# Seven quadrant products in place of eight for the feed-forward input stages of a two-block network on one core

## What is computed

```python
SEQ, D_MODEL, D_FF = 512, 1024, 2816

def swiglu_ffn(x, w_in, w_out):
    gate, up = jnp.split(x @ w_in, 2, axis=-1)      # w_in: 1024 x 5632
    return (jax.nn.silu(gate) * up) @ w_out         # w_out: 2816 x 1024

h = h + 0.5 * swiglu_ffn(rmsnorm(h, norm_ffn1[l]), ffn1_w_in[l], ffn1_w_out[l])
...                                                  # mixer: retention and pooling, or convolution and delta rule
h = h + 0.5 * swiglu_ffn(rmsnorm(h, norm_ffn2[l]), ffn2_w_in[l], ffn2_w_out[l])
```

## Time and profile before

| | |
|---|---|
| median of 3 runs | 2215.12 us (2214.97 to 2216.24) |
| span of the profiled execution | 2213.7 us |
| PE busy | 2198.3 us, 99% of the span |
| DVE busy | 1071.2 us, 48% |
| ACT busy | 748.3 us, 34% |
| POOL busy | 439.2 us, 20% |

### The profile page before, as it was taken

The page is one execution under the profiler, slowest core; times in us unless marked ns, Lnnn a source line. Parts: engine busy times, 40 slices in busy tenths (PEclk is TensorE's granted clock), DMA queues, the critical chain, the costliest instruction groups (busy, mean ns, idle before and its releaser), DMA issues.

```text
span 2213.7 us, 26476 instructions
## 1 busy us (share of the span) xinstructions
PE 2198.3 (99%) x10012; PEld 1820.3 (82%) x10012; DVE 1071.2 (48%) x1126; ACT 748.3 (34%) x1000; POOL 439.2 (20%) x343
## 2 busy tenths in 40 slices
PE   8999999999999999999999999999999999999998
PEld 6888888888777888888888888888788888888887
DVE  6444334453466545444444544443588866444322
ACT  5232222232233334222232422223472354232222
POOL 1222101620123002222211222230002003222101
PEclk9999999999999999999999999999999999999999
DMA  4322234333222232233333223233322123233232
GB/s 147 95 97 101 95 105 133 95 115 100 81 79 74 87 99 99 96 95 95 95 107 111 92 99 95 95 105 105 110 71 67 53 82 95 95 99 100 95 105 96
DMA packets 60255, 213.54 MB, mean 96 GB/s; under 512 B 6688, under 2 KB 9120, under 8 KB 59936
## 3 DMA queue, kind: packets, MB, share of 16 engines
q1 hardware_dynamic: 59616, 209.50, 29.5%
q0 software_dynamic: 288, 2.62, 0.3%
q10 hardware_dynamic: 288, 0.52, 0.1%
HBM read 210.52 MB, written 2.10 MB: 96 GB/s over the span
## 4 chain that ended last, share of the span: by engine, by line
PE 97%; issue 1%; DVE 0%; DMA 0%; POOL 0%; ACT 0%; SPq 0%; POOLq 0%
PE acc L541 30%; PE acc L543 30%; PE acc L542 30%; PE mixb L1022 1%; PE mixb L1045 1%; PE acc L984 1%; PE acc L983 1%; PE acc L982 1%; PE mixb L867 0%; PE acc L878 0%; PE mixb L878 0%; DMA w_raw<-weights 0%; PE acc L867 0%; PE sums L788 0%; PE sums L592 0%
## 5 line engine op out<-in xcount | busy, mean ns | idle before, releaser
L541 PE MATMUL acc<-x_hi,w_hi 128*128 128x512 f32 x2016 | 792.7, 393 | 7.8 <-DVE x_lo L1528 7.8
L543 PE MATMUL acc<-x_hi,w_lo 128*128 128x512 f32 x2016 | 786.0, 390 | 0.0
L542 PE MATMUL acc<-x_lo,w_hi 128*128 128x512 f32 x2016 | 785.7, 390 | 0.0
L541 PEld LDWEIGHTS acc<-x_hi,w_hi 128*128 128x128 f32 x2016 | 379.2, 188 | 86.7 <-DVE x_lo L1528 8.8
L543 PEld LDWEIGHTS acc<-x_hi,w_lo 128*128 128x128 f32 x2016 | 379.0, 188 | 79.7
L542 PEld LDWEIGHTS acc<-x_lo,w_hi 128*128 128x128 f32 x2016 | 379.4, 188 | 77.5
L1509 DVE TENSOR_TENSOR w_lo<-w_raw,w_hi 128x1024 fp32r<-128x1024 f32 x231 | 298.0, 1296 | 232.7 <-ACT w_hi L1095 231.7
L1621 DVE TENSOR_TENSOR w_lo<-w_raw,w_hi 128x1024 fp32r<-128x1024 f32 x160 | 246.3, 1539 | 271.0 <-ACT w_hi L1101 271.0
L1095 ACT ACTIVATE w_hi<-w_raw 128x1024 fp32r<-128x1024 f32 x231 | 242.1, 1054 | 286.6 <-DMA w_raw<-weights 286.6
L541 PE MATMUL acc<-hid_hi,w_hi 128*128 128x512 f32 (+1 forms) x726 | 277.9, 383 | 0.0
L542 PE MATMUL acc<-hid_lo,w_hi 128*128 128x512 f32 (+1 forms) x726 | 277.7, 383 | 0.0
(11 more groups left out here) (363 smaller groups left out, 1749.7 us busy)
## 6 DMA issues: line engine op xcount, KB each, us to landing
w_raw<-weights SPq DMA_DIRECT2D x391, 512.0 KB, 3.4
y_t<-h SPq DMA_DIRECT2D x16, 128.0 KB, 1.8
h<-x_t SPq DMA_DIRECT2D x3, 512.0 KB, 6.8
k1c<-const POOLq DMA_DIRECT2D x1, 1536.0 KB, 9.2
k2c<-const POOLq DMA_DIRECT2D x1, 1024.0 KB, 7.8
h<-x_t ACTq DMA_DIRECT2D x2, 256.0 KB, 4.0
w_raw<-weights SPq DMA_DIRECT2D x1, 384.0 KB, 5.2
cst<-const SPq DMA_DIRECT2D x1, 161.0 KB, 8.4
```

The lines of the kernel that those rows point to most:

```text
L541: pe.matmul(bank, w_hi[:, slot, w], hi, start=start, stop=False)
L542: pe.matmul(bank, w_hi[:, slot, w], lo, start=False, stop=False)
L543: return pe.matmul(bank, w_lo[:, slot, w], hi, start=False, stop=stop)
```

## The change

An input stage now works on a double: two gate tiles and two up tiles of 128 features at once, 11 doubles a part (6 and then 5, `HALVES`). The four weight tiles that face a pair of input tiles are seen as a 2x2 matrix of quadrants, and the tokens are cut into two halves of 256. The 2x2 by 2x2 product is made with seven products of quadrants instead of eight (Winograd's form of Strassen's scheme). So a double has seven blocks of 24 matmuls with 256 columns, named `P1 P6 P2 P7 P5 P4 P3` in their order, where there were four blocks of 24 matmuls with 512 columns.

What this needs besides:

- DVE makes four sums of weight blocks per double (`weight_sum`, s1 to s4, 128x1024 each), and splits seven blocks rather than four.
- The input tiles are combined too: `xc_hi` and `xc_lo` hold seven combinations of 256 tokens for each of four pairs of tiles. `combine` on ACT and DVE makes them once ahead of each part, in place of `x_hi` and `x_lo`.
- Three PSUM areas `r_a`, `r_b`, `r_c` of two half banks hold running sums of products. ACT copies P1 to `f_s`; DVE takes seven steps of 512 elements to get gate and up from the areas (counted by `quad`; `made(d, "u2")` and so on name them). PE may start P7 only when the step `u2` has read `r_b`, P4 after `u3`, P3 after `c22`.
- Silu (ACT), the product `hid_f` (DVE, `hidden`) and `hid_hi` (ACT) are now 128x1024, once per double. POOL makes `hid_lo` alone, one instruction of 128x1024 per double, and `f_mul` is gone; `rstd` enters the up side when the output is added to `h` instead.
- The output stage runs in two passes, after 6 doubles and after 5, in 12 and 10 full blocks; each of the eight tiles is drained and added to `h` in both (`add_tile`, two DVE instructions, where there was one in all).
- Weights have eight slots. The hardware loops are gone, all blocks are written out.

```diff
-PHASES = [("ffn0_in", 2 * KF), ("ffn0_out", 3 * KD), ("pool_in", 4), ...
+PHASES = [("ffn0_in0", 42), ("ffn0_out0", 12), ("ffn0_in1", 35), ("ffn0_out1", 10), ("pool_in", 4), ...
+PRODUCTS = ("p1", "p6", "p2", "p7", "p5", "p4", "p3")
+P1, P6, P2, P7, P5, P4, P3 = range(7)
+B11, B21, B22, T2, U3, U1, U4 = range(7)
+COMBO = (B11, T2, B21, U3, U1, U4, B22)
+HALVES = (6, 5)
...
+NORM_AT = {0: P2, 1: P6, 2: P6, 3: P6}
...
+            def quadrants(f, d, n0, before, fresh):
+                for i, x in enumerate(COMBO):
+                    n = n0 + i
+                    take_block(n)
...
+                    if i == P2:
+                        pe.wait_ge(f_acted, 2 * d + 1)
+                        bank = r_a
+                    if i == P7:
+                        pe.wait_ge(quad, made(d, "u2"))
+                        bank = r_b
+                    if i == P5:
+                        if d:
+                            pe.wait_ge(quad, made(d - 1, "c12"))
+                        bank = r_c
+                    if i == P4:
+                        pe.wait_ge(quad, made(d, "u3"))
+                        bank = r_b
+                    if i == P3:
+                        pe.wait_ge(quad, made(d, "c22"))
+                        bank = r_c
...
+                    for u in range(2):
+                        for k in range(KD // 2):
...
+                            last = product(n, 4 * u + k, bank[:, u, :], xc_hi[:, k, x, :], xc_lo[:, k, x, :],
+                                           opens and k == 0, k == KD // 2 - 1, read_between=True)
+                    last.then_inc(block_done, 1)
...
+            def hidden(d):
+                dve.wait_ge(f_acted, 2 * d + 2)
+                if d:
+                    dve.wait_ge(hid_done, 2 * d)
+                dve.tensor_tensor(hid_f[:, hid_of(d), :], f_up[:, :, :], f_gate[:, :, :], ALU.mult).then_inc(hid_done, 1)
...
+                        before(n0 + P2)
+                        if not fresh:
+                            hidden(d - 1)
+                        split(n0 + P2)
...
+                        prepare(n0 + P7)
...
+                        dve.wait_ge(block_done, n0 + P6 + 1)
+                        dve.tensor_tensor(f_gate[:, :, t2], r_b, f_s[:, :, :], ALU.subtract).then_inc(quad, 1)
+                        prepare(n0 + P5)
...
-                        pool.wait_ge(f_sig_done, q + 1)
-                        pool.tensor_tensor(f_mul[:, u, :], f_sig[:, u, :], rstd[:, :], ALU.mult).then_inc(f_mul_done, 1)
-                        pool.wait_ge(hid_hi_done, q + 1)
-                        pool.tensor_tensor(hid_lo[:, 2 * i + u, :], f_hid[:, u, :], hid_hi[:, 2 * i + u, :].bitcast(F32),
-                                           ALU.subtract).then_inc(hid_done, 1)
+                    pool.wait_ge(normed, WIDE["norm3"] + 1)
                     for m in range(KD):
                         pool.tensor_tensor(h[:, m, :], h[:, m, :], r_one[:, :], ALU.mult).then_inc(h_final, 1)
+                for d in range(sum(HALVES) * f, sum(HALVES) * (f + 1)):
+                    pool.wait_ge(hid_hi_done, d + 1)
+                    pool.tensor_tensor(hid_lo[:, hid_of(d), :], hid_f[:, hid_of(d), :], hid_hi[:, hid_of(d), :].bitcast(F32),
+                                       ALU.subtract).then_inc(hid_done, 1)
```

More of the change, by code:

```diff
@@ new lines, with tile_end, _take @@
+TILE_ENDS = [[m for m in range(8) if OUT_END[p][m] % 8 != 7] for p in range(2)]
+def tile_end(f, p, m):
+    g = OUT_END[p][m]
+    if g % 8 == 7:
+        return "block", FIRST[f"ffn{f}_out{p}"] + g // 8 + 1
+    return "tile", f * (len(TILE_ENDS[0]) + len(TILE_ENDS[1])) + (len(TILE_ENDS[0]) if p else 0) + TILE_ENDS[p].index(m) + 1
+BUFFERS = 8
+RAW, LO, LOADS, LOADED, FREED = {}, {}, [], {}, {}
+_free = {slot: -1 for slot in range(BUFFERS)}
+_times = {slot: 0 for slot in range(BUFFERS)}
+def _take(name, load, slots=BUFFERS):
+    slot = min(range(slots), key=lambda s: (_free[s], s))
+    if load:
+        LOADS.append((slot, _free[slot]))
+        _times[slot] += 1
+        LOADED[name] = (slot, _times[slot])
+    else:
+        FREED[name] = _free[slot]
+    after, _free[slot] = _free[slot], NB
+    return slot
@@ new lines, in out_tiles @@
+            def out_tiles(f, p):
+                first, out0, ds = FIRST[f"ffn{f}_out{p}"], OUT0[f"ffn{f}_out{p}"], [d for d, n0 in doubles(f, p)]
+                for g, (m, k) in enumerate(OUT_SEQ[p]):
+                    if f == 3 and p == 1 and m == KD - 1:
+                        if k == 0:
+                            last_tile(g, first, out0 + m)
+                        continue
+                    n = first + g // 8
+                    if g % 8 == 0:
+                        take_block(n)
+                    if k == 0:
+                        if m < 2:
+                            pe.wait_ge(quad, made(ds[-1], "c11"))
+                        elif m < 4:
+                            pe.wait_ge(quad, made(ds[-1], "c21"))
+                        else:
+                            pe.wait_ge(drained, out0 + m - 3)
+                    if m == 0 and k % 2 == 0:
+                        pe.wait_ge(hid_done, 2 * (ds[0] + k // 2) + 2)
+                    last = product(n, g % 8, acc[m % 4], hid_hi[:, k, :], hid_lo[:, k, :], k == 0, k == 2 * HALVES[p] - 1)
+                    if g % 8 == 7:
+                        last.then_inc(block_done, 1)
+                    elif g == OUT_END[p][m]:
+                        last.then_inc(tile_done, 1)
@@ L651, in last_sum @@
+            def ffn(f):
+                for p in range(2):
+                    for i, (d, n0) in enumerate(doubles(f, p)):
+                        quadrants(f, d, n0, OUT0[f"ffn{f}_in{p}"], i == 0)
+                    out_tiles(f, p)
             def last_sum(t):
@@ L1189, in ffn @@
-                split(first + 2 + LEAD)
-                for u in range(2):
-                    act.wait_ge(drained, out0 + 2 * u + 1)
-                    act.activation(f_sig[:, u, :], f_gate[:, u, :], ACT.Silu).then_inc(f_sig_done, 1)
-                    if u:
-                        split(first + 2 * u + 1 + LEAD)
-                    act.wait_ge(drained, out0 + 2 * u + 2)
-                    act.activation(hid_hi[:, u, :], f_hid[:, u, :], ACT.Copy).then_inc(hid_hi_done, 1)
-                with act.Fori(1, 2 * KF // SLOTS) as i:
-                    turn_of(i)
@@ L2392 @@
     arrays = {
-        "weights": np.concatenate(list(_weights(v))).reshape(NB, P, TILES * P),
+        "weights": np.concatenate([w.reshape(-1, P, TILES * P) for w in _weights(v)]),
         "x_t": np.ascontiguousarray(v["x"][0].T.reshape(KD, P, S).transpose(1, 0, 2)),
```

846 lines of the change are left out of this document (503 added, 343 removed), and 3 rows, old and new, of the table PHASES.

## The result

The changed kernel takes 2302.2 us (median of 4, 2301.74 to 2304.48) where the kernel before takes 2215.3 (2214.97 to 2216.24): 1.039 times as long, 95% interval 1.038 to 1.041. The forecast was 2242, with a range up to 2268. Its direction was right, and its size was 60 us short. The profiled execution has a span of 2299.9 us, against 2213.7.

The account below looks back on a forecast made before the run. PE, busy 99%, was taken as the bound. From 2213.7 us: -71.3 PE's stream, +47.9 ordinary doubles, +24 part 0, +9.2 parts 1 and 3, +17.7 part 2; 2241.2, with 1.4 for the median 2242 us, range 2190 to 2268.

Parts of the forecast that it names:

- What bounds it, and PE's stream: Whole kernel: PE is the bound; input stages' matmuls fall from 957.6 to 886.3 us, 71.3 us less.
- the rival by which each weight load shows: Input stages: weight loads do not overlap, 0.213 us a matmul, 2834 us in all; chance 0.01.
- The ordinary double: 36 doubles: P7 waits for `u2`, delayed by POOL's `hid_lo`; 1.33 us each, 47.9 in all, bounds 0 and 61.
- So 0.7 to 0.9 of what is left.: DVE step starting inside a POOL instruction loses this share of its remainder; the split of P7 loses 1.9 of 2.4 us.
- Eight first doubles, second passes: First doubles after each start have no `hidden`, so no such loss; second passes of output have room on DVE: 0 us.
- Part 0: Start of the first part: input mixing and DVE's order delay the first blocks, 24 us (18 to 30).
- Parts 1, 2 and 3: Starts, counted from the last tile of `h`: 4.6 us each for parts 1 and 3, 17.7 for part 2.
- The products of `h` by `r_one`: Start of part 2: POOL's eight products, moved there from the end of the input stage, cost 6 us.
- The tail: End of the kernel: loses one add of 0.4 us, saves 72 matmuls' fixed 0.013 us; counted as 0.
- POOL misses the split: Rival, ordinary double: POOL starts inside the split of P7 and waits, so P7 is on time; 2194 us, chance 0.22.
- works as meant: Rival, whole kernel: the design works and the starts are hidden too; 2144 us, chance 0.04.
- DVE behind for good: Rival, doubles: DVE's own sum exceeds PE's, 22 us a double; 2262 us, up to 2280; chance 0.12.

Follow-up runs that it names:

- e1: The changed kernel with DVE instead of POOL making `hid_lo`, just ahead of step c12: 2239.6 us.
- e2: The changed kernel with POOL making `hid_lo` in two instructions of 512 elements instead of one of 1024: 2261.9 us.
- e4: The changed kernel with DVE doing the sum s1 after `u2` instead of ahead of the split of P7: 2272.7 us.
- e5: The changed kernel with ACT's rounding of the inner tiles, which releases POOL, moved behind the split of P5's weights: 2239.2 us.
- f4: e1 with DVE instead of POOL adding the squares for the norms ahead of parts 1, 2 and 3: 2220.5 us.
- f1: e1 with ACT rounding the next output block's weights earlier, ahead of the tile's square, in output stages ahead of parts 1 to 3: 2225.4 us.
- f2: e1 with POOL's sums of squares ahead of parts 1 to 3 cut to 16 columns of 512, leaving most out: 2215.5 us.
- g1: e1 with the edits of f1 and f4 together: 2213.6 us, 0.9993 of the kernel before.
- f3: e1 with POOL's eight products of `h` by `r_one` at the start of part 2 cut to 16 columns of 512: 2234.5 us.

## Why the forecast was wrong in size and right in kind

**What bounds it, and PE's stream: right.** 256-column matmuls with a weight load each keep their 0.120 us in the loops: seven blocks of 24 take 20.16 us in e1, 20.14 forecast. The 71.3 us are there in every kernel, and the rival by which each weight load shows (0.213 us a matmul, 2834 us) is out.

**The ordinary double: the mechanism was right, the term mis-sized.** The step that failed: "So 0.7 to 0.9 of what is left." I read three losses as a fraction and took 0.8 of 2.4. They are no fraction. In the rows that I had, the losses are 0.37, 1.09 and 1.07 with 0.51, 1.23 and 1.21 us of POOL's left: each time what is left less 0.14. After the change it is the same: 2.35 left, loss 2.21; in e2 1.24 and 1.11; in e4 and e5 1.75 and 1.61. The DVE instruction does its work when POOL's has ended. For 2.4 us left that makes 2.26, not 1.9; 2.35 were left and 2.21 lost, 0.3 us a double more than forecast. The rest of the 0.46 by which a double was missed is the gap from the end of `u2` to P7 (0.14) and 0.03 for PE's own stream and the order. "Here POOL starts 0.4 inside s1 and loses 0.3" had it on the wrong engine: s1 takes its 1.22, and POOL, which came second, is the one held, by 0.46 (2.86 us where one alone takes 2.40 at 1202.38).

The upper bound, 1.7 us, was exceeded (1.79), because it was built with 0.9 of what is left. e1 and e5 show that the cause is this overlap and its place, not DVE's amount of work: both lose 0 to 0.02 us a double.

The Trainium skill (GPSIMD Engine Reference, Key points) says that POOL shares its SBUF interfaces with DVE. The traces agree and give the size. The same section says that DVE is about twice as fast at elementwise work; here it is 0.61 against 1.29 us for 512 elements, and f4, with 28 such adds moved to DVE, is 19.1 us faster.

**Eight first doubles, second passes: wrong for one of them.** "I take 0 there" held for seven of the eight output passes; the one ahead of part 2 lost 10.8 us. The reason given, a split and two drains per 5.44 us, left out that the tiles of this pass are also mixed, squared and scaled for the next part.

**Part 0: right within its range**, 27.5 for 24 (18 to 30). All kernels have it, also those in which POOL makes no `hid_lo`. What sets it is read from the trace and was not tested: from 24 to 60 us DVE's own row has two waits over 1 us, 1.12 for ACT's rounding and 1.23 for the root.

**Parts 1, 2 and 3: the step that failed is "From the last tile of `h` (T) P1 runs".** I started the clock at T and took T as unchanged. But the mixing of the first three pairs lies ahead of T, in the stage before, and there a pair takes DVE 11.9 us for PE's 10.88 (part 1), 19 for 13.6 (part 2) and 9.1 for 5.44 (part 3). The forecast had a pair at "about 3.7 us" and charged only the last one, without hand-offs and without POOL's sums. f1 prices the hand-offs at 14.3 us, f2 POOL's sums at 24.1. With both mended (g1) part 1 costs 5.2, near the 4.6 that I had without them, and part 2 20.0 for 17.7. Part 3 still costs 14.4, three times the forecast. There g1's DVE works almost without a gap, 8.65 us a pair (the adds at 1830.07, 1838.72 and 1847.38) for PE's 5.44, so that the stage ahead can't hide the mixing, whatever the hand-offs. Without most of the sums, on either engine, it costs 11.0 (f2). That the amount of DVE's work is the bound is read from these rows; no run tests it.

**The products of `h` by `r_one`: right.** 6 us forecast, 5.1 measured in f3.

**The tail**: 0 forecast, 1.7 measured, not followed up. The forecast's "saves 72 matmuls'" is a miscount: 72 matmuls of 256 columns go, but 36 of 512 come, so it is 36 matmuls and 0.5 us.

**The rivals.** POOL misses the split (2194): no, it met it 36 times of 36; the order in which the two met was fixed to hundredths of a microsecond. It as well as "works as meant" (2144) overlooked the starts. "DVE behind for good" is refuted: PE waits once a double, and e1 gives DVE more instructions and loses nothing. The range ended at 2268 because the bounds of the starts were taken from the same incomplete list as their values.

## What to carry to other kernels

Work given to POOL is not off DVE: where both read SBUF, a DVE step that starts second mostly does its work only when POOL's instruction has ended (the exceptions are below). Count POOL's instruction at its full length on DVE's row, unless DVE waits there or reads a PSUM bank, and move its start before you move its work (e5: 63 us for one moved line).

When a new step is made "once ahead of a stage", it lies in the stage before. Cost it there, pair by pair (for each stage with its own count of matmuls per pair), with each wait between two engines that pass the same tile back and forth, and compare with what PE takes for the same tiles.

## What the runs showed that I had not expected

The lock works both ways, and in most meetings its size is exact: whoever starts second, POOL or DVE, lasts its own time plus what is left of the other's less 0.13 to 0.16 us, in the eleven cases of 512 elements or more shown or used above (0.19 for the 256 of L1760), and for 45 splits and sums of weights of the changed kernel that start with over 0.3 us left of a POOL instruction with two inputs. It also holds a DVE step with one SBUF tensor and a column of factors, L1803: 1.62 us at 1234.02 for the 0.49 that it takes in f4, although POOL's instruction (1234.07) is recorded 0.05 us behind it.

It is no law. Two splits of the changed kernel (at 1906.48 and 1915.57) start behind one of POOL's sums and lose nothing, and POOL waits for two DVE steps in a row:

```profile
1905.35 1.21 DVE L1713 TENSOR_TENSOR w_raw<-w_raw 128x1024 f32<-128x1024 f32 x1
1905.44 3.41 POOL L2499 TENSOR_TENSOR sumsq<-sumsq,square 128x512 f32<-128x512 f32 x1 [3.09 <-ACT square L1259]
1906.48 1.21 DVE L1725 TENSOR_TENSOR w_lo<-w_raw,w_hi 128x1024 fp32r<-128x1024 f32 x1
```

In the ordinary double POOL starts 0.62 us inside s1 and is ahead of the next split each time; here it starts 0.09 inside the sum and is not. In f1 ten splits or sums pass POOL in this way. Why is open. And beside POOL's product with one input (L2548, `p_out<-p_sum`) a split loses 0.23 us with 1.25 us of it left (416.75, with POOL's from 416.19 to 418.00), not 1.1.

After some idle times at a start PE's matmuls are further apart, 0.213 us for 256 columns, as at 1.2 GHz, where they are 0.120 at 2.4 GHz:

```profile
1277.31 0.58 PE L660 MATMUL accs<-xc_hi,w_hi 128*128 128x256 f32 x1 [4.29 <-DVE xc_lo L1776]
1277.69 0.41 PE L661 MATMUL accs<-xc_lo,w_hi 128*128 128x256 f32 x1
1277.90 0.41 PE L662 MATMUL accs<-xc_hi,w_lo 128*128 128x256 f32 x1
1278.12 0.41 PE L660 MATMUL accs<-xc_hi,w_hi 128*128 128x256 f32 x1
```

The granted clock is 0.50 of full speed from 1277.7 to 1280.4, where these lie, 0.93 from 1200 to 1400, and 1.00 from 60 to 400. In the first 40 us the spacing tells more than the recorded clock: from 24.63 to 27.41 it is 0.213 too, while the record says 1.00. So a late block at a start is charged twice, by the wait and by a slower block. An estimate of the second charge: stretches of four and more matmuls at the slow spacing add 17.7 us to the changed kernel (181 matmuls) and 1.7 to the one before, out of the 91.5 that the four starts cost; where the next wait would have swallowed the time anyway, they cost less. In the 36 ordinary doubles, with 1.55 us of idle time each, the spacing stayed at 0.120.
